# Squares of three norms summed under the stream ahead of them, GQA gates in two halves, and buffers, tables and loads moved

## The reference

```python
# first block
x = x + (g_pool * pool_mixer + g_attn * window_attention) @ w_out
h = rmsnorm(x, ffn_norm)                                   # norm2
up = causal_depthwise_conv(h @ w_up, conv_w, conv_b)
x = x + (silu(gate) * val) @ w_down
# second block, layer 0 (GQA) and layer 1 (MLA), each:
h = rms_norm(x, w) * (1 + scale(cond)) + shift(cond)       # l0norm, l1norm
q, k, v, g = h @ w_in ...                                  # heads normed, rotated
x = x + gate(cond) * ((attend(q, k, v) * silu(g)) @ w_out)
```

## Time and profile before

| what | value |
|---|---|
| median of 3 runs | 3719.6 us (3718.01 to 3723.22) |
| the profiled execution | 3717.26 us, span 3715.5 us |
| TensorE, VectorE | busy 3420.7 us (92%), 2270.7 us (61%) |
| ScalarE, GpSimd | busy 1836.3 us (49%), 1612.7 us (43%) |
| mean granted TensorE clock | 0.964 of full |
| HBM traffic | 84 GB/s over the span |

### The profile page before, as it was taken

The page is one execution under the profiler, slowest core; times in us unless marked ns, Lnnn a source line. Parts: engine busy times, 40 slices in busy tenths (PEclk is TensorE's granted clock), DMA queues, the critical chain, the costliest instruction groups (busy, mean ns, idle before and its releaser), DMA issues.

```text
span 3715.5 us, 48022 instructions
## 1 busy us (share of the span) xinstructions
PE 3420.7 (92%) x15046; PEld 2692.7 (72%) x15046; DVE 2270.7 (61%) x2620; ACT 1836.3 (49%) x3085; POOL 1612.7 (43%) x980
## 2 busy tenths in 40 slices
PE   7999998999999999899978999998987969999999
PEld 5778876768888887577856777775765647777767
DVE  6794877567676765694056666655257875555552
ACT  3333877041010100432168888823366857877770
POOL 3432544434444353132256666631212326666652
PEclk9998999999999999899989999998998979999999
DMA  2133233212212121134234434332163343323312
GB/s 101 47 123 104 74 77 119 68 40 71 71 57 85 57 85 45 46 114 140 82 66 99 89 70 95 64 105 87 49 227 114 101 121 96 73 52 78 73 37 71
DMA packets 196084, 313.48 MB, mean 84 GB/s; under 512 B 100929, under 2 KB 111681, under 8 KB 195969
## 3 DMA queue, kind: packets, MB, share of 16 engines
q1 hardware_dynamic: 195968, 312.01, 29.5%
HBM read 234.02 MB, written 77.92 MB: 84 GB/s over the span
## 4 chain that ended last, share of the span: by engine, by line
PE 36%; DVE 10%; ACT 5%; issue 4%; DMA 2%; SPq 2%; POOL 1%; DVEq 0%; ACTq 0%; POOLq 0%
PE PB L240 4%; PE PB L241 4%; PE PB L242 4%; PE PMX L1751 4%; PE PD L1792 2%; PE PD L1793 2%; PE PD L1794 2%; PE PMX L240 2%; PE PMX L241 2%; PE PMX L242 2%; DVE gqa_m L1887 1%; PE PD L697 1%; PE PB L1776 1%; PE PB L1775 1%; PE PB L1777 1%
## 5 line engine op out<-in xcount | busy, mean ns | idle before, releaser
L214 POOL TENSOR_TENSOR w_hi<-w_stage,zero 128x1024 fp32r<-128x1024 f32 (+2 forms) x142 | 270.5, 1905 | 1099.2 <-PE PB L242 634.0
L1860 POOL TENSOR_TENSOR gqa_pl<-gqa_pf,gqa_ph 128x512 fp32r<-128x512 f32 (+1 forms) x288 | 371.3, 1307 | 195.9 <-ACT gqa_ph L1833 195.2
L1860 POOL TENSOR_TENSOR mla_pl<-mla_pf,mla_ph 128x512 fp32r<-128x512 f32 x256 | 351.4, 1382 | 235.7 <-ACT mla_ph L1833 231.6
L216 POOL TENSOR_TENSOR w_lo<-w_stage,w_hi 128x1024 fp32r<-128x1024 f32 (+2 forms) x142 | 362.5, 2553 | 11.2
L1497 ACT ACTIVATE conv_in<-PB 128x512 f32<-128x512 f32 x66 | 39.6, 599 | 480.9 <-PE PB L242 475.9
L1887 DVE TENSOR_REDUCE gqa_m<-PMX 128x1 f32<-128x1280 f32 (+1 forms) x160 | 203.8, 1274 | 119.0 <-PE PMX L1751 118.1
L1887 DVE TENSOR_REDUCE mla_m<-PMX 128x1 f32<-128x1280 f32 x128 | 190.3, 1487 | 91.5 <-PE PMX L1751 91.1
L1828 ACT ACTIVATE mla_pf<-PB 128x512 f32<-128x512 f32 x320 | 189.8, 593 | 97.1 <-PE PB L1777 83.6
L1828 ACT ACTIVATE gqa_pf<-PB 128x512 f32<-128x512 f32 (+1 forms) x352 | 201.7, 573 | 50.9 <-PE PB L1780 46.8
L1833 ACT ACTIVATE gqa_ph<-gqa_pf 128x512 fp32r<-128x512 f32 (+1 forms) x352 | 215.6, 613 | 13.8
L1833 ACT ACTIVATE mla_ph<-mla_pf 128x512 fp32r<-128x512 f32 x320 | 202.3, 632 | 12.6
(11 more groups left out here) (404 smaller groups left out, 10052.7 us busy)
## 6 DMA issues: line engine op xcount, KB each, us to landing
mod_w<-in_w_mod SPq DMA_DIRECT2D x48, 512.0 KB, 3.5
w_stage<-in_w_up SPq DMA_DIRECT2D x44, 512.0 KB, 3.4
w_stage<-in_w_go SPq DMA_DIRECT2D x24, 512.0 KB, 4.0
gqa_k<-kh_d SPq DMA_DIRECT2D x32, 320.0 KB, 5.0
gqa_q<-qh_d SPq DMA_DIRECT2D x32, 320.0 KB, 7.5
w_stage<-in_w_down SPq DMA_DIRECT2D x24, 384.0 KB, 3.6
qh_d<-heads_qh SPq DMA_DIRECT2D x32, 256.0 KB, 2.1
ql_d<-heads_ql SPq DMA_DIRECT2D x32, 256.0 KB, 2.3
```

Of the source, the lines that this page charges most:

```text
L214: pool.tensor_tensor(w_hi[s][:, 0:st.cols], w_stage[s][:, 0:st.cols], z, ALU.add).then_inc(w_hi_done, 1)
L216: pool.tensor_tensor(w_lo[s][:, 0:st.cols], w_stage[s][:, 0:st.cols], w_hi[s][:, 0:st.cols].bitcast(F32), ALU.subtract).then_inc(w_split, 1)
L1860: eng.tensor_tensor(self.PL[k % 4][:, 0:n], self.PF[k % 4][:, 0:n], self.PH[k % 4][:, 0:n].bitcast(F32), ALU.subtract).then_inc(self.lo_dv ...
```

## The change

**Norms.** `NormAhead` replaces `Norm` for norm2, l0norm and l1norm. While the stream ahead of the norm runs, ScalarE squares each tile of `X` as soon as its residual is written, and GpSimd adds the squares to `ACC` (between its weight splits); where a chunk isn't written by the stream (the context in `down3`) its squares come first. TensorE makes one sum for each chunk: of chunk 0 inside the last units of the stream or at its end, of the others inside the next projection. Ln and Exp go to `ACC` in place. The phase for the sums is gone: scaling runs beside the projection's first units.

**Gates.** `l0_g` becomes `l0_g1` (4 panels, right behind l0norm, before `l0_q`) and `l0_g2` (4 panels, where all 8 were), with six banks in place of three. The rotation tables of layer 0 are loaded ahead of the gates.

**Modulation.** `mods_dve` moves to earlier units of a pair, `mods_finish` to before the last stream of the FFN and before the last unit of `l0_out`.

**Attentions.** The constants of the first buffers are set in the stage before, those of the second after the first maxima. The first four maxima alternate between `PMX` and `PBX` (the three banks of `PB` as one tensor). MLA's first queries are loaded in the last turn of `l1_qg`.

**Layer 1.** `rotate_kr` is spread between keys 12 to 18. A load of the table set of Ln and Exp stands at the start of each turn of `l1_qg`, and its last turn makes the four heads earlier and ends with gates.

```diff
+    ("l0_g1", "l0_w_g", 0, 4, 1024, 3),
     ("l0_q", "l0_w_q", 0, 8, 1024, 3), ("l0_k", "l0_w_k", 0, 2, 1024, 3), ("l0_v", "l0_w_v", 0, 2, 1024, None),
-    ("l0_g", "l0_w_g", 0, 8, 1024, 3), ("l0_out", "l0_w_o", 0, 8, 1024, 3),
+    ("l0_g2", "l0_w_g", 4, 4, 1024, 3), ("l0_out", "l0_w_o", 0, 8, 1024, 3),
...
-        def split_stream(pool, st):
+        def split_stream(pool, st, norm=None):
+            if norm is not None:
+                norm.pool_begin(pool)
             def body(i, last):
                 for s in range(2):
+                    if last and s and norm is not None:
+                        for x in range(norm.nch - 1):
+                            norm.pool_add(pool, i, s, x)
                     if not last:
                         split_panel(pool, st, s, i + (st.p0 // 2 + 1), i * (2 * st.upp) + (st.u0 + (s + 1) * st.upp),
                                     i * 2 + 2 + s)
                     elif st.next is not None:
                         done = st.u0 + sum(st.units_of[:st.panels - 1 + s])
                         split_panel(pool, st.next, s, st.next.p0 // 2, done, s)
+                    if norm is not None:
+                        for x in range(norm.nch - 1 if last and s else 0, norm.nch):
+                            norm.pool_add(pool, i, s, x)
...
+                    for c in range(1, len(chunks)):
+                        if sums is not None and k == 3 * c:
+                            sums(c)
...
+                            if tail is not None and last and (u, k) == tail:
+                                sums(0)
...
+            def act_squares(self, act):
+                U, upp = 2 * self.nch, self.st.upp
+                def square(i, u):
+                    s, c = u // self.nch, self.order[u % self.nch]
+                    o, n = self.chunks[c]
+                    if c < upp:
+                        act.wait_ge(unit_evac, i * (2 * upp) + (EVAC_CREDIT + self.st.u0 + s * upp + c + 1))
+                    act.wait_ge(self.acc, i * U + (self.a0 + u))
+                    act.activation(SQ[u % 2][:, 0:n], X[:, bass.ds(i * 2 + s, 1), o:o + n].rearrange("p o n -> p (o n)"),
+                                   ACT.Square).then_inc(self.sq, 1)
+                def body(i, last):
+                    for u in range(U):
+                        if last and u == U - 1:
+                            act.preload_act_table_set(LN_EXP)
+                            self.act_rsqrt(act, 0)
+                        square(i, u)
...
+            def pool_begin(self, pool):
+                if self.a0 == 1:
+                    pool.sem_inc(self.acc, 1)
+                pool.wait_ge(units_done, self.st.u0)
+                pool.memset(ACC[:, :], 0.0).then_inc(self.acc, 1)
+            def pool_add(self, pool, i, s, x):
+                U = 2 * self.nch
+                u, c = s * self.nch + x, self.order[x]
+                o, n = self.chunks[c]
+                pool.wait_ge(self.sq, i * U + (self.j0 + u + 1))
+                pool.wait_ge(self.acc, i * U + (self.a0 + u + 1))
+                pool.tensor_tensor(ACC[:, o:o + n], ACC[:, o:o + n], SQ[u % 2][:, 0:n], ALU.add).then_inc(self.acc, 1)
...
+            def pe_sum(self, pe, c):
+                o, n = self.chunks[c]
+                if c == 2:
+                    pe.wait_ge(self.rs, 2 * self.c0 + 2)
+                pe.wait_ge(self.acc, self.a0 + 1 + (KT - 1) * self.nch + self.order.index(c) + 1)
+                pe.matmul(SIDE[c % 2][:, 0:n], ones[:, :].bitcast(F32), ACC[:, o:o + n], start=True, stop=True).then_inc(self.sum, 1)
...
+            def act_rsqrt(self, act, c):
+                o, n = self.chunks[c]
+                r = ACC[:, o:o + n]
+                act.wait_ge(self.sum, self.c0 + c + 1)
+                act.activation(r, SIDE[c % 2][:, 0:n], ACT.Ln, bias=EPS, scale=1.0 / D).then_inc(self.rs, 1)
+                act.wait_ge(self.rs, 2 * (self.c0 + c) + 1)
+                act.activation(r, r, ACT.Exp, scale=-0.5).then_inc(self.rs, 1)
+            def act(self, act):
+                act.preload_act_table_set(LN_EXP)
+                for c, (o, n) in enumerate(self.chunks):
+                    for k in range(KT):
+                        j = self.j0 + c * KT + k
+                        act.wait_ge(self.t, j + 1)
+                        act.activation(self.HH[:, k, o:o + n], self.T[k % 2][:, 0:n], ACT.Identity,
+                                       bias=self.shift(k, c)).then_inc(self.hi, 1)
+                        if k == 6 and c + 1 < len(self.chunks):
+                            self.act_rsqrt(act, c + 1)
...
+            def dve(self, dve):
+                for c, (o, n) in enumerate(self.chunks):
+                    dve.wait_ge(self.rs, 2 * (self.c0 + c) + 2)
+                    def low(k):
+                        j = self.j0 + c * KT + k
+                        dve.wait_ge(self.hi, j + 1)
+                        dve.scalar_tensor_tensor(out=self.HL[:, k, o:o + n], in0=self.T[k % 2][:, 0:n],
+                                                 scalar=self.shift(k, c), in1=self.HH[:, k, o:o + n].bitcast(F32),
+                                                 op0=ALU.add, op1=ALU.subtract).then_inc(self.lo, 1)
+                    for k in range(KT):
+                        j = self.j0 + c * KT + k
+                        if j >= 2:
+                            dve.wait_ge(self.lo, j - 1)
+                        dve.scalar_tensor_tensor(out=self.T[k % 2][:, 0:n], in0=X[:, k, o:o + n], scalar=self.gain(k, c),
+                                                 in1=ACC[:, o:o + n], op0=ALU.mult, op1=ALU.mult).then_inc(self.t, 1)
+                        if k:
+                            low(k - 1)
+                    low(KT - 1)
...
-                if u % 2:
+                if u % 2 == 0:
...
+            l0norm.pe_sum(pe, 0)
...
+            l0norm.act_squares(act)
...
+                if g == MODS_IN:
+                    mods_finish(dve, 0)
...
+                    project(pe, self.st, self.chunks, HH, HL, self.banks, ready=norm.ready(pe), first="together",
+                            sums=lambda c: norm.pe_sum(pe, c))
...
+            def const_sp(self, sp, q):
+                for a, d in enumerate((krh_d, krl_d)):
+                    sp.dma_start(self.K[q][a][64:96, :].bitcast(F32), d).then_inc(self.const[q], 16)
+            def const_dve(self, dve, q):
+                dve.memset(self.V[q][0][:, :, 64:128].bitcast(F32), 1.0).then_inc(self.const[q], 1)
+                dve.memset(self.V[q][1][:, :, 64:128].bitcast(F32), 0.0).then_inc(self.const[q], 1)
+                dve.memset(self.K[q][0 if self.mla else 1][self.row:self.row + 1, :].bitcast(F32), 1.0)\
+                   .then_inc(self.const[q], 1)
...
-                    maxima(0, 0, 0, t, t, t == 0, 0)
+                    maxima(0, 0, 0, t, t, t == 0, 0, (PMX, PBX)[t % 2], CR_R - min(t, 1))
...
-                    maxima(0, 0, t, 0, t)
+                    maxima(0, 0, t, 0, t, (PMX, PBX)[t % 2])
                 diag(0, 0, 0, 3)
+                self.const_dve(dve, 1)
...
-        gates0 = SiluGates("l0_gate", tmp, STREAM["l0_g"], CHUNKS_ALL, 3)
+        gates1 = SiluGates("l0_gate2", tmp, STREAM["l0_g2"], CHUNKS_ALL, 6)
...
-                if u % 3 < 2:
-                    mods_dve(dve, i * 2 + (16 + u // 3), u % 3, mod_w0, cond_s0)
+                if u < 4:
+                    mods_dve(dve, i * 2 + (16 + u // 2), u % 2, mod_w0, cond_s0)
+                if u == 4 and isinstance(i, int):
+                    mods_finish(dve, 1)
...
+                    if c == 0 and k in (3, 6):
+                        l1norm.pe_sum(pe, k // 3)
...
             for x in range(12, 24):
+                rotate_kr(dve, x - 12)
                 key(x)
-            rotate_kr(dve)
...
+                if x == 18:
+                    sp.wait_ge(kr_link, 7)
...
+            mla.const_sp(sp, 0)
...
+                if last:
+                    for b in range(2):
+                        sp.wait_ge(heads_ql.stored[b], 64 + 16 * heads_ql.j0)
+                    mla.load_q(sp, 0, 0)
...
+                if last:
+                    head(0)
+                    head(1)
+                    mean(0)
+                    head(2)
+                    gate(0, 2)
+                    mean(1)
+                    head(3)
+                    gate(2, 6)
+                    mean(2)
+                    gate(6, 10)
+                    mean(3)
+                    gate(10, 16)
+                    return
                 head(0)
...
+                act.preload_act_table_set(LN_EXP)
...
+            mla.const_dve(dve, 0)
...
-            split1.pe(pe, STREAM["out"], CHUNKS_X, 4)
+            split1.pe(pe, STREAM["out"], CHUNKS_X, 4, lambda c: norm2.pe_sum(pe, c), (3, 5))
             end_phase(pe, "pe")
-            norm2.pe(pe)
-            end_phase(pe, "pe", wait=False)
             ffn_pe(pe)
             end_phase(pe, "pe")
-            l0norm.pe(pe)
```

(5 more changed lines are left out.)

205 lines of the change are left out of this document (120 added, 85 removed).

## The result

The changed kernel takes 3602.6 us (median of 4, 3598.7 to 3613.3), the kernel before beside it 3721.4: a ratio of 0.9685, 95% interval 0.966 to 0.971. The forecast was 3597 with 3569 to 3636. The profiled execution was the longest of the four, 3613.3 (span 3611.4), so its trace shows 104.1 us less than the one of before, not 119.

The account below looks back on a forecast made before the run. TensorE, busy 3420.7 of 3715.5 us, bounds the kernel; only its stretches without reference products or at lower clock can shrink. Terms of 19, 17, 35, 9.5, 6, 20 and 16.5 sum to 123 us: 3597 us, range 3569 to 3636.

Parts of the forecast that it names:

- norm2: Norm ahead of the FFN: cost falls from 34.3 to 15.3 us, 19 us saved (15 to 23).
- rival A: Norms: the clock doesn't come back where TensorE follows VectorE tile by tile; 30 us, total 3627; chance 0.15.
- Layer 0: Norm ahead of layer 0: cost falls from 45.8 to 29.1 us, 17 us saved (12 to 24).
- layer 1's norm: Norm ahead of layer 1: GpSimd in time, cost falls from 46.4 to 11.5 us, 35 us saved (29 to 38).
- Key/value end: End of the key/value stage: rotation steps spread between keys, 3.5 us of delay counted, 6 us saved (2 to 8).
- Query/gate loop: Layer-1 query/gate loop: one table load removed from the path, less slow clock; 2.9 x 7 = 20 us (9 to 27).
- rival B: Query/gate loop doesn't gain: loads put in again or VectorE becomes the bound; 15 to 20 us less, 3614; chance 0.12.
- Attention starts: Starts of GQA and MLA: earlier memsets and loads, two buffers; 9.5 us (7 to 10.5) and 16.5 us (11 to 21).
- rival C: Streams ahead of the norms: GpSimd's 64 additions starve the weight splits, kernel slower than before; chance 0.01.
- the gates in two halves: Layer 0's gates: as many products, no gate unit waited for a bank before, so 0 us.

Follow-up runs that it names:

- the late split: GpSimd's split of the last projection's first two panels moved from the last query/gate turn to MLA's start, against the changed kernel: 3603.5 us.

## Why the prediction came out right, and where it didn't

The saved time is where the prediction put it, with one wait that it had not seen. The sizes came out less well (104.7 and 113.9 us by the traces for 123), and that the total came within 6 us of 3597 is partly luck.

**Norms.** The pace is as forecast: one sum a chunk, VectorE in front, products 0.43 us apart only for the first 6 us (rival A is out; its 30 us would show in all three). norm2 gave 15.4 for 19, the low end: 18.6 in its stage, less 1.1 for the sum on TensorE, and 1.1 each in `down0` and `down2`. There the modulation sums now lie one unit earlier and the next weights come 0.9 us late for TensorE; with the old norm put back these two losses stayed, so they don't come from the squares and are put down to the moved sums. Layer 0 gave 16.4 for 17; its scaling starts 11.7 us after the last product for a forecast of 11.6.

**The step that failed is layer 1's norm**, "a panel has 13.8 us, so GpSimd is in time". On average it is: 4.7 of split and 2.5 additions. At the last panel it isn't. The split waits for the same panel's last product, takes 5.3 us beside the modulation sums, and four additions of 1.3 to 2.3 us come behind it; the sum stands 30 products ahead of the stream's end (the expectation above says 25), waits 3.48 us, and leaves a slow start. The stream is 6.1 us longer for it, 5.4 net of the shorter hole; with the sum last, the term is 30.9 us, in its range. I had counted the sum's own duration and not where it is queued. 4 us are left to the forecast's 35, and no run takes them apart. In that run VectorE's second and third scaling instructions last 2.84 and 1.21 us beside a split, for 0.75 (2.6 us, where 1 was counted), and `l1_a` takes 103.2 us from its first to its last product, against 97.6 before.

**Key/value end.** I kept 3.5 us of delay by the steps between the keys. The stream got 0.7 to 1 us longer than before the change, and the stop went entirely, since no one but VectorE and SyncE waits for a key's last steps until MLA. That makes 9.7 and 10.5 us for a forecast of 6.

**Query/gate loop.** 20.2 for 20, hole and slow products as forecast. VectorE now has no slack at all in a turn: rival B's mechanism is real, it begins just where the forecast ended. The prediction's 4.6 us a turn in which VectorE isn't busy belonged to the old turn of 27.3; in the new one 1.45 are left, all short steps. That TensorE's own cycle (22.94 us of products and the 1.49 us stop) and VectorE's are both 24.43 is, as far as the runs show, chance.

**Attention starts.** The second buffer brings the first scores 4.64 us sooner in each, for 4.5. MLA's stop stays at 12.1 to 12.4 us for a forecast of 9.5: VectorE ends 7.2 to 7.5 us behind the last product, not 5, as GpSimd's split slows its last head, then stores and the end of the phase. In the first profile MLA's own length had 5 us of chance against it.

**GpSimd and VectorE together.** The Trainium skill, "GPSIMD Engine Reference" (its table of the engine), says they contend for shared SBUF interfaces when VectorE has two SBUF inputs or works in a two-port mode. The trace agrees that they contend: 0.69 against 2.71 us for one multiplication is the plainest row. Of two instructions with one operand the shuffle isn't slowed (0.72) and the cast is (0.42 to 1.15); no run here shows why. The effect was weighed at 3.5 us in the norms and not at all elsewhere, and is worth more: the late split alone gave 5.9 at MLA's start, and it fills VectorE's turn in the loop. The key/value end and the two losses of norm2 have other causes. On table loads the Trainium skill, "ScalarE: Activation LUTs" (What ACT_TABLE_LOAD costs), adds a drain of 1380 ns to each switch. It is not seen here: the next instruction follows 0.01 us behind the load, and TensorE's stop fell by 1.28 us (2.77 to 1.49), the load alone.

Two figures of the prediction are wrong without changing its outcome. The high ends add up to 151.5, not 150.5. And rival C's "no two-input instruction on GpSimd takes over 1.7 us for 512 columns" misreads the trace of before, where single ones take up to 2.2 us (mean 1.38).

Left open: how much of the second buffer's 4.64 us each attention keeps to its end, and the gates in two halves, which I had at nothing and didn't try alone. Layer 0's stage came out within 1 us of its forecast with them in it.

## What to carry to other kernels

Work put on an idle engine must be followed to its last panel: there it meets the next stream's work, and an instruction that waits for it in the middle of TensorE's queue pays for the whole backlog (3.48 us here, 15.70 with the additions doubled). Compare stages from last product to last product, not holes, since a short hole may only hand its wait to the products behind it. And when a loop gets faster, count the slack of the second engine: here filling TensorE's stop only moved it, because VectorE had none, and 4.9 us of its turn were the price of GpSimd's splits.
